# A mixture-of-experts encoder layer: the second expert bias, the last job's rows, the end of the first job and the empty slots

## What is computed

```python
logits = ht @ w_router + b_router                 # 32 experts
top_v, top_i = lax.top_k(logits, 4)
gate = jax.nn.softmax(top_v, axis=-1)
# per expert e, for the tokens that chose it:
gu = xb @ w_gu[e] + b_gu[e]                       # 1024 -> 2048
g = jnp.minimum(gu[:, :1024], 7.0)
lin = jnp.clip(gu[:, 1024:], -7.0, 7.0)
act = g * jax.nn.sigmoid(1.702 * g) * (lin + 1.0)
ys = act @ w_down[e] + b_down[e]                  # 1024 -> 1024
y = segment_sum(ys * gate_of_row, token_of_row)   # back to the tokens
x = rmsnorm(x + y)
```

## Time and profile before

| | us |
|---|---|
| median of 3 executions (1668.89 to 1673.39) | 1672.84 |
| the profiled execution | 1673.61 |
| its span in the profile | 1671.8 |
| PE busy | 1608.1 (96%) |
| DVE busy | 1284.0 (77%) |
| ACT busy | 1099.7 (66%) |
| POOL busy | 350.9 (21%) |
| transfers, mean over the span | 285 GB/s |

### The profile page before, as it was taken

How to read it: one execution, slowest core, us unless ns; L and a number is a source line. 1 busy time by engine, 2 the same in 40 slices (tenths; PEclk the granted TensorE clock), 3 DMA queues, 4 the chain that set the end, 5 groups by cost and what they waited for, 6 DMA issues and landing times.

```text
span 1671.8 us, 21874 instructions
## 1 busy us (share of the span) xinstructions
PE 1608.1 (96%) x7703; PEld 1184.1 (71%) x7703; DVE 1284.0 (77%) x1004; ACT 1099.7 (66%) x1036; POOL 350.9 (21%) x277
## 2 busy tenths in 40 slices
PE   7999999999996999999999999999999999999993
PEld 6877788888874776777776777776777776777772
DVE  3756635334687999888899898899898899898881
ACT  5356752233355877777777777777777777777762
POOL 1000046000032222322222322222322222322210
PEclk9999999999997999999999999999999999999997
DMA  7210003325666999999999999999999999999963
GB/s 285 75 62 20 1 20 125 96 81 181 269 264 250 358 378 368 371 368 368 381 377 374 367 373 366 382 374 373 371 366 366 382 376 377 369 365 367 386 241 119
DMA packets 101910, 476.00 MB, mean 285 GB/s; under 512 B 11065, under 2 KB 11601, under 8 KB 69073
## 3 DMA queue, kind: packets, MB, share of 16 engines
q1 hardware_dynamic: 93504, 448.18, 69.7%
q0 software_dynamic: 8032, 27.24, 7.0%
q10 hardware_dynamic: 336, 0.08, 0.0%
HBM read 456.69 MB, written 19.66 MB: 285 GB/s over the span
## 4 chain that ended last, share of the span: by engine, by line
PE 94%; DVE 3%; ACT 1%; DMA 1%; issue 1%; POOL 0%; ACTq 0%; DVEq 0%; POOLq 0%
PE ps L1658 28%; PE ps L1679 14%; PE ps L1661 14%; PE ps L1684 7%; PE ps L1387 6%; PE ps L1388 6%; PE ps L1389 6%; PE ps L1414 5%; PE ps L1517 2%; PE ps L1650 2%; PE ps L1491 2%; DVE l_w L1175 1%; PE ps L1670 1%; PE ps L1482 1%; PE ps L1587 0%
## 5 line engine op out<-in xcount | busy, mean ns | idle before, releaser
L798 ACT ACTIVATE h_w<-a_w 128x2048 fp32r<-128x2048 f32 x384 | 731.7, 1915 | 255.8 <-PE ps L1661 179.3
L1175 DVE TENSOR_TENSOR l_w<-a_w,h_w 128x2048 fp32r<-128x2048 f32 x384 | 869.6, 2292 | 38.3 <-ACT h_w L798 36.2
L1658 PE MATMUL ps<-h_w,xt_hi 128*96 128x512 f32 x1024 | 287.2, 402 | 1.3 <-DVE xt_lo L1311 1.3
L1658 PE MATMUL ps<-h_w,xt_lo 128*96 128x512 f32 x1024 | 279.5, 394 | 0.0
L1661 PE MATMUL ps<-l_w,xt_hi 128*96 128x512 f32 x1024 | 278.7, 393 | 0.0
L947 POOL TENSOR_TENSOR mark_sb<-ones 1x1 f32<-1x1 f32 x96 | 97.7, 1018 | 844.7 <-ACT y_sb L847 833.8
L1658 PEld LDWEIGHTS ps<-h_w,xt_lo 128*96 128x96 f32 x1024 | 166.2, 162 | 71.8
L1661 PEld LDWEIGHTS ps<-l_w,xt_hi 128*96 128x96 f32 x1024 | 165.9, 162 | 71.6
L1658 PEld LDWEIGHTS ps<-h_w,xt_hi 128*96 128x96 f32 x1024 | 163.5, 162 | 69.9 <-DVE xt_lo L1311 1.5
L1679 PE MATMUL ps<-h_w,at_hi 128*96 128x512 f32 x512 | 168.1, 409 | 0.0
L1679 PE MATMUL ps<-h_w,at_lo 128*96 128x512 f32 x512 | 160.4, 394 | 0.0
(11 more groups left out here) (231 smaller groups left out, 1697.2 us busy)
## 6 DMA issues: line engine op xcount, KB each, us to landing
a_w<-in_w_gate_up SPq DMA_DIRECT2D x256, 1024.0 KB, 7.7
a_w<-in_w_down SPq DMA_DIRECT2D x128, 1024.0 KB, 6.3
w_raw<-in_w_in SPq DMA_DIRECT2D x8, 2048.0 KB, 7.9
w_raw<-in_w_out SPq DMA_DIRECT2D x2, 2048.0 KB, 7.7
x_sb<-in_x SPq DMA_DIRECT2D x4, 512.0 KB, 6.1
w_raw<-in_w_in SPq DMA_DIRECT2D x2, 1024.0 KB, 10.4
w_raw<-in_w_mem_kv SPq DMA_DIRECT2D x1, 2048.0 KB, 14.7
x<-in_x SPq DMA_DIRECT2D x4, 512.0 KB, 5.2
```

Of the source, the lines that this page charges most:

```text
L798: nc.scalar.activation(h_w[m % H_SLOTS][:], a_w[m % A_SLOTS][:], ACT.Copy).then_inc(wh_done, 1)
L1175: nc.vector.tensor_tensor(l_w[m % A_SLOTS][:], a_w[m % A_SLOTS][:], h_w[m % H_SLOTS][:].bitcast(F32), ALU.subtract).then_inc(wl_done, 1)
L1658: nc.tensor.matmul(ps[0:SLOTS, n, :], x_part[:, k, :], w_h[:, n * COLS:(n + 1) * COLS], start=False, stop=False)
```

## The change

It has four parts.

1. `down` has no bias matmuls and `name_dn` is gone. Instead DVE builds, once, the gate weight of every expert for every token (`gate_e`), PE transposes it after the slot tables in job 0 (`gate_t`, copied by ACT), and at the end PE multiplies it in float32 with the table of the second biases (`down_bias`, 32 x 1024).
2. The last job's rows aren't added in memory. ACT and DVE split them (`y_hi_last`, `y_lo_last`), and PE adds them to their tokens by a one-hot matrix (`token_hot`) in the same banks as the bias product. DVE then adds these banks to the loaded rows. The loads wait only for the scatter of the last but one job. The Sqrt table of ACT is asked for ahead of the last `down`'s end.
3. In job 0 ACT takes job 1's tokens between Relu and Sigmoid. DVE does three splits, `clamp`, the minimum of the gate half into `y_sb` (after which PE may write the banks), `low_xt(1)`, one split, the two products, and then the other splits.
4. The indirect transfers get a bound of 511 and drop rows above it; so POOL clears both gather buffers once, ahead of the first gather.

```diff
-        bias_down = sb("bias_down", [96, D], BF16, 200 * KIB)
+        gate_t = sb("gate_t", [N_EXP, SEQ], F32, 200 * KIB)
...
+        gate_e = sb("gate_e", [P, TB, N_EXP], F32, 190 * KIB + 512)
...
+        down_bias = sb("down_bias", [N_EXP, D], F32, 160 * KIB)
+        y_hi_last = sb("y_hi_last", [SLOTS, D], F32R, 170 * KIB)
+        y_lo_last = sb("y_lo_last", [SLOTS, D], F32R, 180 * KIB)
+        token_hot = sb("token_hot", [SLOTS, TB, P], F32R, 184 * KIB)
+        row_f = sb("row_f", [SLOTS, 1], F32, 186 * KIB)
+        xf_squares = sb("xf_squares", [P, D], F32, 0)
+        LAST_BANK = (0, 2, 6, 4)
...
+            sp.dma_start(down_bias[:], b_down[0]).then_inc(down_bias_in, 16)
+            sp.wait_ge(added, pairs_but_one * 32 + 32)
...
-            def name_dn(j):
-                nc.scalar.activation(expert_dn[:], job_hot_b[:, bass.ds(j, 1)].to_broadcast([96, SLOTS]), ACT.Copy).then_inc(expert_dn_ready, 1)
...
-            def sigmoid(j):
+            def sigmoid(j, between=None):
 
                 nc.scalar.activation(sg_sb[:].rearrange("p (h n) -> p h n", h=2), ps[0:SLOTS, 0:2, :], ACT.Relu, bias=limits[0:SLOTS, 0:1],
                                      scale=-1.0).then_inc(under_limit, 1)
+                if between:
+                    between()
...
+            act.wait_ge(gate_e_ready, 1)
             for m in (6, 7):
                 moe_high(0, m)
+            act.wait_ge(gate_t_ps, 1)
+            nc.scalar.activation(gate_t[:], ps[0:N_EXP, 4, :], ACT.Copy).then_inc(gate_t_ready, 1)
             for p in range(KD):
                 if p == 1:
                     act.wait_ge(hot_b_ready, 1)
                     name_gu(1)
                 if p == KD - 1:
                     wait_part(act, 0, KD - 1)
-                    sigmoid(0)
+                    sigmoid(0, lambda: take_xt(1))
                 moe_high(0, p + H_LEAD)
-            take_xt(1)
...
-                            name_dn(j)
...
-            name_dn(pairs_but_one * 2 + 1)
             take_act(pairs_but_one * 2 + 1)
             take_y(pairs_but_one * 2, 0)
             keep_gate(pairs_but_one * 2 + 1, 1)
+            nc.scalar.activation(mark_act[:], ones[0:1, 0:1], ACT.Sqrt).then_inc(gate_kept, 1)
+            act.wait_ge(gate_kept, pairs_but_one * 2 + 3)
             wait_part(act, pairs_but_one, stream(0, PARTS + DN_PARTS - 1))
-            take_y(pairs_but_one * 2 + 1, 1)
-
-            for t in range(TB):
-                act.wait_ge(xf_in[t], 16)
-                nc.scalar.activation(ps[:, 2 * t:2 * t + 2, :], xf[:, t, :].rearrange("p (a n) -> p a n", a=2), ACT.Square,
-                                     accum_out=f_ss[:, t:t + 1]).then_inc(fsq_done, 1)
+            nc.scalar.activation(y_hi_last[:].rearrange("p (h n) -> p h n", h=2), ps[0:SLOTS, 4:6, :], ACT.Copy,
+                                 scale=y_gate[:, 1:2]).then_inc(y_hi_ready, 1)
+
+            def root_of_sum(t):
                 act.wait_ge(fms_ready, t + 1)
                 nc.scalar.activation(f_rt[:, t:t + 1], f_ms[:, t:t + 1], ACT.Sqrt).then_inc(frt_ready, 1)
+
+            for t in range(TB):
+                act.wait_ge(xf_ready, t + 1)
+                if t:
+                    act.wait_ge(fsq_done, t)
+                nc.scalar.activation(xf_squares[:], xf[:, t, :], ACT.Square, accum_out=f_ss[:, t:t + 1]).then_inc(fsq_done, 1)
+                if t:
+                    root_of_sum(t - 1)
+            root_of_sum(TB - 1)
...
-            bias_pieces = [(bias_gu[:, 0:D], b_gate_up[0][:, 0:D]), (bias_gu[:, D:2 * D], b_gate_up[0][:, D:2 * D]), (bias_down[:], b_down[0])]
+            bias_pieces = [(bias_gu[:, 0:D], b_gate_up[0][:, 0:D]), (bias_gu[:, D:2 * D], b_gate_up[0][:, D:2 * D])]
...
-                                             in_offset=bass.IndirectOffsetOnAxis(ap=rows, axis=0)).then_inc(xg_in[s], 16)
+                                             in_offset=bass.IndirectOffsetOnAxis(ap=rows, axis=0),
+                                             bounds_check=SEQ - 1, oob_is_err=False).then_inc(xg_in[s], 16)
 
             def add_rows(s):
                 nc.gpsimd.indirect_dma_start(out=x_rows, out_offset=bass.IndirectOffsetOnAxis(ap=sum_row[:, s:s + 1], axis=0),
-                                             in_=y_sb[:], in_offset=None, compute_op=ALU.add).then_inc(added, 16)
+                                             in_=y_sb[:], in_offset=None, bounds_check=SEQ - 1, oob_is_err=False,
+                                             compute_op=ALU.add).then_inc(added, 16)
...
+            for s in range(2):
+                nc.gpsimd.memset(xg[s][:], 0.0).then_inc(xg_clear, 1)
+            pool.wait_ge(xg_clear, 2)
...
-            for b in range(2):
-                j = pairs_but_one * 2 + b
-                mark(j * 3 + 2)
-                keep_row(sum_row[:, b:b + 1], j)
-                pool.wait_ge(rows_kept, pairs_but_one * 4 + 2 + b)
-                mark(j * 3 + 3)
-                scatter(j, b)
-            pool.wait_ge(added, pairs_but_one * 32 + 48)
+            j = pairs_but_one * 2
+            mark(j * 3 + 2)
+            keep_row(sum_row[:, 0:1], j)
+            pool.wait_ge(rows_kept, pairs_but_one * 4 + 2)
+            mark(j * 3 + 3)
+            scatter(j, 0)
+            keep_row(sum_row[:, 1:2], j + 1)
+            pool.wait_ge(added, pairs_but_one * 32 + 32)
...
+                step.link(nc.vector.tensor_tensor(place_hot[:], one_hot[:], dest_vals[:, :, 1].rearrange("p (t e k) -> p t e k", t=TB, e=1)
+                                                  .to_broadcast([P, TB, N_EXP, TOP_K]), ALU.mult))
+                nc.vector.tensor_reduce(gate_e[:], place_hot[:], AX_X, ALU.add).then_inc(gate_e_ready, 1)
...
-            for p in range(KD):
-                if p == KD - 1:
-                    wait_part(dve, 0, p)
-                    clamp(0)
-                moe_low(0, p + LOW_LEAD)
-                if p == KD - 1:
-                    activate(0)
+            for m in range(LOW_LEAD, LOW_LEAD + 3):
+                moe_low(0, m)
+            wait_part(dve, 0, KD - 1)
+            clamp(0)
+            dve.wait_ge(under_limit, 1)
+            nc.vector.tensor_scalar(y_sb[:].rearrange("p (h n) -> p h n", h=2), ps[0:SLOTS, 0:2, :], LIMIT, None, ALU.min).then_inc(gs_ready, 1)
             low_xt(1)
+            moe_low(0, LOW_LEAD + 3)
+            dve.wait_ge(sg_ready, 1)
+            dve.wait_ge(gs_ready, 1)
+            step.link(nc.vector.tensor_tensor(sg_sb[:], sg_sb[:], y_sb[:], ALU.mult))
+            dve.wait_ge(l_ready, 1)
+            nc.vector.scalar_tensor_tensor(out=act_sb[:], in0=act_sb[:], scalar=1.0, in1=sg_sb[:],
+                                           op0=ALU.add, op1=ALU.mult).then_inc(act_ready, 1)
+            for m in range(LOW_LEAD + 4, LOW_LEAD + KD):
+                moe_low(0, m)
...
+            dve.wait_ge(at_ps, pairs_but_one * 2 + 2)
+            dve.wait_ge(rows_kept, pairs_but_one * 4 + 3)
+            nc.vector.tensor_copy(row_f[:], sum_row[:, 1:2]).then_inc(row_f_ready, 1)
+            dve.wait_ge(row_f_ready, 1)
+            for t in range(TB):
+                nc.vector.tensor_scalar(token_hot[:, t, :], counter[0:SLOTS, :], float(t * P), row_f[:, 0:1], ALU.add,
+                                        ALU.is_equal).then_inc(token_hot_ready, 1)
+            dve.wait_ge(y_hi_ready, 1)
+            nc.vector.scalar_tensor_tensor(out=y_lo_last[:].rearrange("p (h n) -> p h n", h=2), in0=ps[0:SLOTS, 4:6, :], scalar=y_gate[:, 1:2],
+                                           in1=y_hi_last[:].bitcast(F32).rearrange("p (h n) -> p h n", h=2), op0=ALU.mult,
+                                           op1=ALU.subtract).then_inc(y_lo_ready, 1)
             dve.wait_ge(fgain_in, 16)
-            for t in range(TB):
+            def add_last(t):
+                dve.wait_ge(xf_in[t], 16)
+                dve.wait_ge(last_ps, t + 1)
+                v = xf[:, t, :].rearrange("p (h n) -> p h n", h=2)
+                nc.vector.tensor_tensor(v, v, ps[:, LAST_BANK[t]:LAST_BANK[t] + 2, :], ALU.add).then_inc(xf_ready, 1)
+            def mean(t):
                 dve.wait_ge(fsq_done, t + 1)
                 nc.vector.tensor_scalar(f_ms[:, t:t + 1], f_ss[:, t:t + 1], 1.0 / D, EPS, ALU.mult, ALU.add).then_inc(fms_ready, 1)
+            def norm(t):
                 dve.wait_ge(frt_ready, t + 1)
                 step.link(nc.vector.reciprocal(f_rstd[:, t:t + 1], f_rt[:, t:t + 1]))
                 nc.vector.scalar_tensor_tensor(out=xf[:, t, :], in0=xf[:, t, :], scalar=f_rstd[:, t:t + 1], in1=final_gain[:],
                                                op0=ALU.mult, op1=ALU.mult).then_inc(out_ready, 1)
+            add_last(0)
+            add_last(1)
+            for t in range(TB):
+                mean(t)
+                if t + 2 < TB:
+                    add_last(t + 2)
+                norm(t)
...
+                    pe.wait_ge(gate_e_ready, 1)
+                    for t in range(TB):
```

(46 more changed lines are left out.)

## The result

| | before | after |
|---|---|---|
| median, us | 1670.87 (4 executions, 1668.77 to 1673.39) | 1658.28 (4 executions, 1657.9 to 1658.54) |
| ratio, 95% interval | | 0.9926 [0.9910, 0.9943] |
| the profiled execution, its span | 1673.61, 1671.8 | 1658.54, 1656.7 |

The change makes the kernel 12.6 us faster by the medians and 15.1 us by the two spans. The forecast was 21.7 us. The time lies in the stated range (1646.5 to 1659), but not in the 1647 to 1656 that the working gave to the forecast's own case.

The account below looks back on a forecast made before the run. PE was taken to bound the steady jobs, with both ends bound by chains across engines. Parts of -14.0, -5.5, -2.2 and 0 sum to -21.7 us, giving a forecast of 1651.5 us, range 1646.5 to 1659.

Parts of the forecast that it names:

- the forecast's own case: Whole kernel: all four parts as worked out, 1651.5 us, small errors 1647 to 1656; chance 0.75.
- Rival B: Tail: PE runs at the lower clock, end at T+27.4, 5.6 us more, 1657.1 us; chance 0.10.
- C: Job 1's early start is given back because DVE or ACT meets PE again, at most 5.5 us, 1657.0; chance 0.07.
- Part 4: Tail after the last weight matmul: 21.8 us instead of 24.0, so -2.2 us.
- part 3: End of job 0: job 1's first weight matmul 6.15 us earlier, PE loses about 0.6 once; sum -5.5 us.
- Part 1: Every down loses its pair of bias matmuls, 0.43 us in each of 32; with ACT's copy -14.0 us.
- rival D: Steady jobs: transfers are the bound after all, a job stays at 35.87 us, 1665.3 us; chance 0.04.
- Part 2: Indirect transfers: skipping empty slots is off the path, 0 us; the new POOL memsets are hidden with 1.1 us left.
- the one above: PE's 2.24 us idle at 1632 to 1634.5, after which the clock fell; the new tail's wait was put at 0.9 us.
- T: End of the last weight matmul; the span was forecast to end at T + 21.8 instead of T + 24.0.

Follow-up runs that it names:

- old order: Kernel after with part 3 undone, so ACT and DVE work in their earlier order at the end of job 0: 1667.05 us.
- the late copy: Kernel after with ACT's copy of the gate sums (gate_t) in job 0 placed three splits later: 1650.43 us.
- the last kernel: Kernel after with late gate_t copy, bias products partly ahead of the last down, one-pass over 96 stacked rows, and no unread products: 1643.82 us.
- a pause of 0.89 us with 96 rows: Kernel after with the tail's plain float32 bias products over 96 stacked rows instead of 32, without unread filler products: 1650.65 us.
- the gap filled: Kernel after with four unread products between the first bias pair and the first rows of the last job: 1652.26 us.
- the biases moved: Kernel after with two bias pairs ahead of the last down, the third right behind it, the fourth after three blocks' rows: 1649.33 us.
- one-pass products: Kernel after with the tail's bias products in one pass of rounded float32, still over 32 rows: 1644.61 us.
- 96 rows with the fill: Kernel after with plain float32 bias products over 96 stacked rows and four unread products behind the first bias pair: 1645.28 us.

## Why the prediction was right or wrong

**Inside the range, but not by the forecast's own case.** The time is 6.8 us above the forecast. The range holds it only because its upper end had been moved from 1656 to 1659 to take in rivals B and C, each given 0.10 or less; what happened is close to B's 1657.1. Part 4 came out 7.8 us worse than the forecast and part 3 brought 1.5 us more, so two errors cancel in part, and that is luck.

**Part 1 held.** 13.1 us in 31 jobs and 0.43 in the first are 13.5, forecast 14.0. A steady job of 35.46 with PE busy all the time, no wait for a transfer: rival D is out.

**Part 2 held.** 0, by the run without the bound. The two memsets took 1.85 us together and POOL was still idle 1.29 us behind them, where 1.1 was forecast.

**Part 3 had the right mechanism and was undersized.** Without the bias pair of job 0's `down` the stretch became 7.0 us shorter, its new wait at job 2 included; forecast 5.5. The biases could start at 509.53 (510.0 forecast), the weight matmuls followed them by 1.37 us instead of 1.7, and PE's wait for `xt_lo` at job 2 was 0.18 instead of 0.6: 1.2 us together. The run in the old order gives 7.1. (The working's Relu at 507.7 has a slip, 503.58 and 3.8 are 507.4; it came at 507.05.) That the new stall of ACT sets the gain was in the working, and the late copy showed what it costs: 3.3 us.

**Part 4 failed, and the step is "by the rows the tail stays at the upper level, since the wait is under half of the one above".** Up to the first block the working holds: `y_hi` T+1.15 (1.2), `y_lo` T+2.5 (2.5), first rows T+3.8 (3.5). The pause was even shorter than forecast, 0.70 us. But I asked only how long PE would pause, and never whether a product with 32 rows counts as one with 96 or 128. It does not: last rows at T+20.2 instead of T+11.5, end at T+29.6 instead of T+21.8. With 96 rows the block costs 2.65 us (forecast 2.64) and the tail 21.15 us, 0.65 under the forecast, so the clock's level was the main error. Two small ones stand beside it: 1.73 ns for each of 512 columns are 0.89 us, not the 0.86 of the working, and a pair over 32 rows took 1.91 us at the upper level instead of 1.72.

**Rival B named the level and not the cause.** Its last rows (T+19.7) were 0.5 early; a block took 5.7 us once the clock was down, not 5.1 (twice 2.64 would be 5.3). Its end (T+27.4) was 2.2 early, since behind the last sum three norms still stand and not one (1648.74, 1650.55, 1652.37 by the chain). Its mechanism was a burst with waits between, for which the Trainium skill stands (TensorE: Matmul & The Clock Gate, section HAM oscillation). The trace agrees in one place: after 2.14 us of waiting the last kernel's first products run at the lower level (0.60 on the mean of 1624 to 1628). Elsewhere it does not cover what is seen: in the kernel after the wait ends at T+2.6 and PE is busy without a break until T+20, at 0.50 from T+4.5 on; and a pause of 0.89 us with 96 rows leaves it at 1.00. With the gap filled the fall came later (T+8 by its windows instead of T+4.5), so the wait sets at most when it falls, and the rows decide that it falls and stays down.

## What to carry to other kernels

Ahead of a tail or any stage of small products, look at how many rows of the array they use: here a pair of products over 32 rows in each block took the clock to half, for itself and for the wide products beside it. Stack independent pieces (copies of a high and a low part, several terms of a sum) into one contraction. When a step moves work from a chain of engines onto PE, price it at both levels of the clock, and put what doesn't depend on the late operand into a wait that PE has anyway. When two traces are compared, look first at the granted clock at the start of the stretch: 1.4 of the 4.7 us of the late copy were not the edit's.

## What the runs showed that I had not expected

- PE busy for all of each 4 us stretch from 1632 to 1644 us at a granted clock of 0.50, with two of six products of each block over 32 rows; at 1.00 with the same products over 96 rows. Yet 3.6 us of 32-row products alone, ahead of the last `down` with the biases moved, left it at 1.00. The tail of the kernel before has no products at all, so no row there showed it.
- The same wait does not always take the clock down. PE waits 2.08 us for `y_sb` ahead of the last `down` in nine of the traces; the clock fell behind it in six (0.67 to 0.76 in the lowest window of 4 us) and stayed at 1.00 in three (late copy, one-pass products, 96 rows with the fill). Behind T it fell at once after 2.14 us in the last kernel, and only some 2.6 us after a pause of 1.95 in the one-pass kernel. What decides stays open.
- Executions of the same kernel differ by some 5 us (1649.2 and 1649.5, then 1655.0 and 1655.3 for the filled gap). Between the two traces with 96 rows 4.7 us were spread over the stages ahead of job 0, the end of job 0 and the last `down`, places where the clock falls in one and not in the other; what makes an execution take the one wasn't tried.
